# Layer boundaries run token tile by token tile, with the next features staged between the granules

## What is computed

```python
def rms_norm(x, w):
    y = xf * lax.rsqrt(jnp.mean(xf * xf, axis=-1, keepdims=True) + NORM_EPS)
    return (y * w.astype(jnp.float32)).astype(x.dtype)
...
h = x
for layer in range(DEPTH):
    u = rms_norm(h, mix_norm_pre[layer])
    u = even_mixer(u, ...) if layer % 2 == 0 else odd_mixer(u, ...)
    h = h + rms_norm(u, mix_norm_post[layer])
    u = swiglu(rms_norm(h, ffn_norm_pre[layer]), w_gate, w_up, w_down)
    h = h + rms_norm(u, ffn_norm_post[layer])
# second block: hn = rmsnorm(h, norm_gain[i]); proj = hn @ w_in[i] ...
```

## Time and profile before

| | us |
|---|---|
| median of 3 runs | 2949.03 (2949.02 to 2949.35) |
| the profiled execution, device time | 2949.33 |
| its span in the trace | 2947.5 |
| PE busy with matmuls | 2873.4 (97% of the span) |
| DVE busy | 1656.1 (56%) |
| ACT busy | 1409.6 (48%) |

### The profile page before, as it was taken

The page is one execution under the profiler, slowest core; times in us unless marked ns, Lnnn a source line. Parts: engine busy times, 40 slices in busy tenths (PEclk is TensorE's granted clock), DMA queues, the critical chain, the costliest instruction groups (busy, mean ns, idle before and its releaser), DMA issues.

```text
span 2947.5 us, 37450 instructions
## 1 busy us (share of the span) xinstructions
PE 2873.4 (97%) x15082; PEld 2379.9 (81%) x15082; DVE 1656.1 (56%) x2078; ACT 1409.6 (48%) x1802; POOL 25.2 (1%) x43
## 2 busy tenths in 40 slices
PE   8999989999999999999999999999999999999998
PEld 6888768788888888878887878888888887888886
DVE  5786855644544444564445554554444567786555
ACT  5554475544444444454446454444444445455444
POOL 0000000000000000000000000000000000000000
PEclk9999999999999999999999999999999999999999
DMA  6543325565555555555552655555555654444553
GB/s 238 174 142 114 115 100 202 171 200 188 185 193 192 190 195 185 190 171 197 186 188 83 199 184 191 190 187 192 193 189 190 204 186 139 149 151 170 194 176 129
DMA packets 255846, 516.84 MB, mean 175 GB/s; under 512 B 8528, under 2 KB 8752, under 8 KB 254688
## 3 DMA queue, kind: packets, MB, share of 16 engines
q1 hardware_dynamic: 252896, 501.61, 51.4%
q0 software_dynamic: 2816, 13.33, 1.4%
HBM read 511.76 MB, written 2.10 MB: 174 GB/s over the span
## 4 chain that ended last, share of the span: by engine, by line
PE 93%; DVE 4%; ACT 2%; issue 1%; DMA 0%; SPq 0%; ACTq 0%; DVEq 0%
PE acc L481 85%; DVE ar L1850 1%; ACT ar L1148 1%; PE side L548 1%; PE side L685 1%; PE side L678 1%; DVE wlo L1862 1%; PE side L807 1%; DVE ar L1853 1%; PE side L576 0%; DMA raw<-in_ev_w_in 0%; ACT L1148 0%; DVE u L1850 0%; PE side L951 0%; PE side L991 0%
## 5 line engine op out<-in xcount | busy, mean ns | idle before, releaser
L1862 DVE TENSOR_TENSOR wlo<-raw,whi 128x1024 fp32r<-128x1024 f32 x948 | 1154.4, 1224 | 1086.3 <-ACT whi L1159 1084.9
L1159 ACT ACTIVATE whi<-raw 128x1024 fp32r<-128x1024 f32 x948 | 998.5, 1060 | 1164.2 <-PE acc L481 1162.8
L481 PE MATMUL acc<-whi,xh 128*128 128x512 f32 x3008 | 823.7, 396 | 2.7 <-ACT whi L1159 2.5
L481 PE MATMUL acc<-wlo,xh 128*128 128x512 f32 x3008 | 806.5, 390 | 0.4
L481 PE MATMUL acc<-whi,xl 128*128 128x512 f32 x3008 | 806.5, 390 | 0.0
L481 PEld LDWEIGHTS acc<-wlo,xh 128*128 128x128 f32 x3008 | 564.9, 188 | 121.1 <-DVE wlo L1862 2.9
L481 PEld LDWEIGHTS acc<-whi,xl 128*128 128x128 f32 x3008 | 565.8, 188 | 119.9
L481 PEld LDWEIGHTS acc<-whi,xh 128*128 128x128 f32 x3008 | 555.8, 189 | 114.3 <-issue 3.3
L481 PE MATMUL acc<-whi,hTh 128*128 128x512 f32 x784 | 212.0, 392 | 0.0
L481 PE MATMUL acc<-wlo,hTh 128*128 128x512 f32 x784 | 209.8, 389 | 0.1
L481 PE MATMUL acc<-whi,hTl 128*128 128x512 f32 x784 | 209.6, 389 | 0.0
(11 more groups left out here) (267 smaller groups left out, 1265.7 us busy)
## 6 DMA issues: line engine op xcount, KB each, us to landing
raw<-in_ffn_w_gate SPq DMA_DIRECT2D x88, 1024.0 KB, 5.1
raw<-in_ffn_w_up SPq DMA_DIRECT2D x88, 1024.0 KB, 5.1
raw<-in_ffn_w_down SPq DMA_DIRECT2D x88, 1024.0 KB, 5.0
raw<-in_ev_w_in SPq DMA_DIRECT2D x56, 1024.0 KB, 5.1
raw<-in_od_w_in SPq DMA_DIRECT2D x48, 1024.0 KB, 5.1
raw<-in_w_in SPq DMA_DIRECT2D x32, 1024.0 KB, 5.2
raw<-in_ev_w_out SPq DMA_DIRECT2D x16, 1024.0 KB, 5.0
raw<-in_od_w_out SPq DMA_DIRECT2D x16, 1024.0 KB, 5.0
```

Source lines behind the costliest of these rows:

```text
L481: mm = pe.matmul(acc[2 * pair + t][:], x[:, k0 + j, t * P:t * P + P], w[:, ring, j], start=start and j == 0, stop=stop and j == 1)
L1159: act.activation(whi[:, place % RING], raw_granule(place), ACT.Copy).then_inc(S("hi_done"), 1)
L1862: dve.tensor_tensor(wlo[:, place % RING], raw_granule(place), whi[:, place % RING].bitcast(F32), ALU.subtract).then_inc(S("lo_done"), 1)
```

## The change

At the four boundaries:

- On PE the last two granules of the last chunk of ev_out, dn0b, od_out and dn1b are not run one after the other but as `by_tile`: all twelve matmuls of tile 0 (both granules, three sweeps of two), then all twelve of tile 1. Tile 0's end raises the new semaphore `tile_done`; tile 1's part raises `used` for each granule.
- ACT and DVE enter `lead` after the split of granule 1 of the user layer instead of granule 2 (`lead_at` 1). There the chain is run tile by tile: square, sum, root, reciprocal of tile 0, then h of tile 0 for chunks 0 and 1, then the same for tile 1. Only features of rounds 0 and 1 are made in `lead`.
- PE transposes tile 0 of rounds 0 and 1 on its own, then tile 1 (`open_stream`); rounds 2 and 3 stand before granule 1, rounds 4 and 5 before granule 3, rounds 6 and 7 before granule 4 (`STREAM_AT`, keys are PE's j).
- ACT makes the `xh` of those rounds after its splits of granules 2, 4 and 5 (j - 1 in `STREAM_AT`). DVE makes h of chunk 2 and the `xl` of rounds 4 and 5 after its split of granule 4, and h of chunk 3 and the `xl` of rounds 6 and 7 after its split of granule 5 (`rest`).
- A semaphore `ab_copied` is merged into `ab_done`, and counts of `ssum_done`, `rmsu_done`, `rstdu_done` are doubled, one for each tile.

The diff, cut to its core (s_in is done as od_in is, and feed_forward likewise):

```diff
@@ -76,6 +76,8 @@
 GATE_AT = {3: (0, 1), 4: (2,), 5: (3,), 6: (4,), 7: (5,)}
 LEAD = 7
 STATS = 5
+STREAM_AT = {1: (2, 3), 3: (4, 5), 4: (6, 7)}
+STREAM_READY = (3, 4, 6, 8)
...
+                        if name in POST and c == CHUNKS[name] - 1 and j >= per - 2:
+                            if j == per - 1:
+                                by_tile(name, pair, lhs_h, lhs_l)
+                            yield
+                            continue
                         granule(g, g % RING, pair, lhs_h, lhs_l, 2 * j, j == 0, j == per - 1, low)
                         yield
+
+            def by_tile(name, pair, lhs_h, lhs_l):
+                per = KTS[name] // 2
+
+                def sweep(n, t, x, w, stop=False):
+                    g = gran(name, CHUNKS[name] - 1, per - 2 + n)
+                    k0 = 2 * (per - 2 + n)
+                    for j in range(2):
+                        mm = pe.matmul(acc[2 * pair + t][:], x[:, k0 + j, t * P:t * P + P], w[:, g % RING, j],
+                                       start=False, stop=stop and j == 1)
+                    return mm
+
+                for t in range(TT):
+                    for n in range(2):
+                        g = gran(name, CHUNKS[name] - 1, per - 2 + n)
+                        if t == 0:
+                            pe.wait_ge(S("hi_done"), g + 1)
+                        sweep(n, t, lhs_h, whi)
+                        sweep(n, t, lhs_l, whi)
+                        if t == 0:
+                            pe.wait_ge(S("lo_done"), g + 1)
+                        mm = sweep(n, t, lhs_h, wlo, stop=n == 1)
+                        if t:
+                            mm.then_inc(S("used"), 1)
+                        elif n:
+                            mm.then_inc(S("tile_done"), 1)
...
-                        pe.wait_ge(S("h_done"), 8 * n + 2 * (r // 2) + 2)
+                        pe.wait_ge(S("h_done"), 8 * n + (STREAM_READY[r // 2] if n < 4 else 2 * (r // 2) + 2))
...
+            def open_stream(name, src):
+                n = ("up0a", "od_in", "up1a", "s_in").index(name)
+                base = 8 * TOF[name]
+                banks = [claim(side[r], "xl_done", 2 * (base + r) + 2) for r in range(2)]
+                for t in range(TT):
+                    pe.wait_ge(S("h_done"), 8 * n + (STREAM_READY[0] if t else 1))
+                    for k in range(4):
+                        mm = pe.transpose(banks[k // 2][:, k % 2 * TOK + t * P:k % 2 * TOK + t * P + P],
+                                          src[:, t, k * P:k * P + P], ident)
+                        if t and k % 2:
+                            mm.then_inc(S("tof_ready"), 1)
+
             def features_use(name, src=None):
 
                 def use(c, j):
                     if c == 0:
-                        if src is not None and j < 3:
+                        if name in ("up0a", "od_in", "up1a", "s_in"):
+                            if j == 0:
+                                open_stream(name, src)
+                            elif j in STREAM_AT:
+                                to_features(name, src, STREAM_AT[j])
+                        elif src is not None and j < 3:
                             to_features(name, src, (range(4), range(4, 6), range(6, 8))[j])
                         pe.wait_ge(S("xh_done"), 2 * (8 * TOF[name] + j + 1))
...
-            def granules(name, evac, lead, aside=None, after=2):
+            def granules(name, evac, lead, aside=None, after=2, lead_at=None):
...
-                        if j == min(after, per - 1):
-                            if c == 0:
-                                lead()
-                            else:
-                                evac(c - 1)
+                        if c == 0 and j == min(after if lead_at is None else lead_at, per - 1):
+                            lead()
+                        if c and j == min(after, per - 1):
...
-            def square_out(name, c):
+            def square_out(name, c, tiles=range(TT)):
                 n = 8 * POST[name] + 2 * c
-                if name[:2] != "dn":
-                    chunk_done(name, c)
                 pair = (CHUNK0[name] + c) % 2
-                for t in range(TT):
+                for t in tiles:
                     if name[:2] == "dn":
                         act.wait_ge(S("u_done"), 8 * int(name[2]) + 2 * c + t + 1)
                         src = u[:, t, c * CH:c * CH + CH]
                     else:
+                        if c == 3 and t == 0:
+                            act.wait_ge(S("tile_done"), POST[name] + 1)
+                        else:
+                            chunk_done(name, c)
                         src = acc[2 * pair + t][:]
                     if n + t:
                         act.wait_ge(S("sq_done"), n + t)
                     if n + t and POST[name] and c == 0:
-                        act.wait_ge(S("ssum_done"), POST[name])
+                        act.wait_ge(S("ssum_done"), 2 * POST[name])
                     run(at(14336, CH), src, ACT.Square, "sq_done", accum_out=ss[:, 4 * t + c:4 * t + c + 1])
...
-            def rms_out(name):
-                act.wait_ge(S("ssum_done"), POST[name] + 1)
-                if POST[name]:
-                    act.wait_ge(S("rstdu_done"), POST[name])
-                run(rms_u, ssum, ACT.Sqrt, "rmsu_done", scale=1.0 / DM, bias=EPS)
+            def roots_out(name, user):
+                before_root()
+                for t in range(TT):
+                    square_out(name, 3, (t,))
+                    act.wait_ge(S("ssum_done"), 2 * POST[name] + t + 1)
+                    if POST[name]:
+                        act.wait_ge(S("rstdu_done"), 2 * POST[name] + t - 1)
+                    run(rms_u[:, t:t + 1], ssum[:, t:t + 1], ACT.Sqrt, "rmsu_done", scale=1.0 / DM, bias=EPS)
+                features_hi(user, range(2))
...
-                            if first and m == 0 and j == 2:
+                            if first and m == 0 and j == (1 if name[3] == "a" else 2):
                                 lead()
+                            if first and m == 0 and name[3] == "a" and j - 1 in STREAM_AT:
+                                features_hi(name, STREAM_AT[j - 1])
...
-                    before_root()
-                    square_out(before, 3)
-                    rms_out(before)
-                    features_hi(f"up{l}a")
+                    roots_out(before, f"up{l}a")
...
+            def summed(name, c, t):
+                pair = (CHUNK0[name] + c) % 2
+                x = u[:, t, c * CH:c * CH + CH]
+                if c == 3 and t == 0:
+                    dve.wait_ge(S("tile_done"), POST[name] + 1)
+                else:
+                    chunk_done(name, c)
+                dve.wait_ge(S("half_done"), 8 * (int(name[2]) + 1))
+                tt(x, acc[2 * pair + t][:], x, ALU.add, "u_done")
+
+            def gained(name, c, tiles=range(TT)):
                 n = POST[name]
                 if n < 4 and c == 0:
                     dve.wait_ge(S("grow_in"), 16 * (n + 1))
@@ -2190,13 +2251,10 @@
                         dve.wait_ge(S("h_done"), 8 * n)
                 pair = (CHUNK0[name] + c) % 2
                 cl = slice(c * CH, c * CH + CH)
-                if name[:2] == "dn":
-                    l = int(name[2])
-                    chunk_done(name, c)
-                    dve.wait_ge(S("half_done"), 8 * (l + 1))
-                    for t in range(TT):
-                        tt(u[:, t, cl], acc[2 * pair + t][:], u[:, t, cl], ALU.add, "u_done")
-                for t in range(TT):
+                if name[:2] == "dn" and c < 3:
+                    for t in tiles:
+                        summed(name, c, t)
+                for t in tiles:
                     dve.wait_ge(S("sq_done"), 8 * n + 2 * c + t + 1)
                     src = u[:, t, cl] if name[:2] == "dn" else acc[2 * pair + t][:]
                     tt(u[:, t, cl], src, grow[:, cl], ALU.mult, "ug_done")
@@ -2204,24 +2262,48 @@
             def into_stream(name, user):
 
                 n = POST[name]
-                dve.wait_ge(S("sq_done"), 8 * n + 8)
-                if n:
-                    dve.wait_ge(S("rmsu_done"), n)
-                dve.tensor_reduce(ssum, ss.rearrange("p (t c) -> p t c", t=TT), AX_X, ALU.add)\
-                    .then_inc(S("ssum_done"), 1)
-                dve.wait_ge(S("rmsu_done"), n + 1)
-                dve.reciprocal(rstd_u, rms_u).then_inc(S("rstdu_done"), 1)
-                dve.wait_ge(S("rstdu_done"), n + 1)
-                dve.wait_ge(S("ug_done"), 8 * n + 8)
+
+                def root(t):
+                    if name[:2] == "dn":
+                        summed(name, 3, t)
+                    dve.wait_ge(S("sq_done"), 8 * n + 6 + t + 1)
+                    if n:
+                        dve.wait_ge(S("rmsu_done"), 2 * n - 1 + t)
+                    dve.tensor_reduce(ssum[:, t:t + 1], ss[:, 4 * t:4 * t + 4], AX_X, ALU.add).then_inc(S("ssum_done"), 1)
```

(56 more changed lines are left out.)

75 lines of the change are left out of this document (34 added, 41 removed).

## The result

| | us |
|---|---|
| median before, same chip | 2949.19 (2949.02 to 2951.3) |
| median after | 2972.24 (2968.62 to 2973.78) |
| ratio | 1.0071, interval 1.0059 to 1.0082 |
| span of the profiled execution | 2970.6, before 2947.5 |

The forecast was 2960.0 with a range of 2950 to 2968: right in sign and in where it happens, too low by 12 us and outside its range. First the page and PE's waits of the changed kernel (in it `granule` is line 483, `by_tile` 533, `to_features` 581, `open_stream` 592, DVE's helper for h and `xl` 1905, ACT's for `xh` 1198 and for `whi` 1209).

A forecast was written before the change was run, and what follows sets the result against it. PE was taken as busy nearly throughout, so only its boundary waits could pay. Shifts of +1.25, +2.4, +0.4 and +4.95 (+9.0), plus +2.1 for the clock, on the median 2949.0 gave 2960 us, range 2950 to 2968.

The forecast's parts named there:

- What bounds, and the yardstick: PE busy nearly throughout; boundaries measured by granule 7's start after Z, the last full sweep's end; each loses 6.4 to 8.0 us.
- The early chain: Tile 0's chain starts 2.73 us earlier; granule 0 starts at Z + 3.8 (ev_out, od_out) or Z + 5.6 (dn0b, dn1b).
- The moved h's: h of chunks 2 and 3, behind splits 4 and 5, makes PE wait before granules 3 and 4: 0.8 and 2.4 us first.
- `whi` at granule 6: At each boundary ACT's statistics delay split 6, so PE waits 1.2 us, plus 0.3 for `wlo`.
- The sum at full clock: Granule 7's shifts over the four boundaries, +1.25, +2.4, +0.4 and +4.95, together +9.0 us.
- The clock: Low clock after the stop in the two dn boundaries, 1.05 us each: +2.1, bounds 0 and +4.2.
- Rival (d): Clock falls again at granules 3 and 4 of each boundary, +1 to +2 each: 2964 to 2972 us, chance 0.12.
- (a): The gain survives, late h's come in time; boundaries at 25.5, 27.3, 25.5, 27.3: 2938 us, chance 0.10.
- (b): Break-even: half of the 0.8 + 2.4 + 1.5 per boundary is absorbed: about 2950 us, range 2944 to 2954, chance 0.15.
- the +13: Reading that transposes do not count as PE activity, so the low clock comes at every boundary.

The follow-up runs named there:

- after_warm: The changed kernel plus idle matmuls, whose results nobody reads, in PE's waits for h and first features at the boundaries: 2960.35 us, ratio 1.0031.
- h_early: The changed kernel with one move undone, h of chunks 2 and 3 made ahead of the split of granule 2: 2950.03 us, ratio 0.9994.
- before_again: The kernel before, run once more unchanged for its trace: 2951.27 us.
- early6_warm: h_early with the statistics one granule later and idle matmuls in the waits ahead of granule 0: 2941.71 us, ratio 0.9966; again 2941.85.
- before_warm: The kernel before with 18 or 21 idle matmuls in the one long wait for h at each boundary: 2944.82 us, ratio 0.998.
- after_again: The changed kernel, run once more unchanged: 2971.37 us, ratio 1.0065.

## Why the prediction was right, and where it was wrong

**What bounds, and the yardstick: right.** The work between boundaries did not move by 0.1 us.

**The early chain: right.** Granule 0 at Z + 3.8 and 5.6, in the trace 3.78, 5.74, 3.78, 5.74. The part of it that is `by_tile` is worth 7.5 us.

**The moved h's: right in place and size.** In the first and third boundary 0.8 + 2.4 were forecast, in the second 0.65 + 2.24; 0.48 + 2.06, 0.46 + 2.05 and 0.50 + 2.07 came in these three, and 2.50 + 2.34 in the fourth, where 2.65 + 4.1 were forecast. The 2.34 was short because granule 3 in front of it took 4.3 us at the low clock (its sweeps begin at 2479.12, the next granule's transposes wait from 2483.6) and DVE caught up meanwhile; with the clock held full, granule 7 of the fourth boundary is at 35.89, forecast 35.6. For `whi` at granule 6 1.2 were forecast and 1.07 came. The sum at full clock was +9.0; the four boundaries of after_warm have +9.6, single ones off by up to 0.3. h_early shows the cause by itself: 21 us back from moving four instructions of DVE in each boundary.

**The clock: this step failed, as a term of the sum.** It took +2.1, with bounds of 0 and +4.2: one fall behind the stop ahead of granule 0 in the two dn boundaries, 1.05 us each, and nothing anywhere else. The span of after's profile is 23.1 us over that of before, where the forecast had 11.1; it divides like this:

| | forecast | measured |
|---|---|---|
| boundaries at full clock (after_warm less before) | 9.0 | 9.6 |
| clock in the boundaries (after less after_warm) | 2.1 | 7.3 |
| outside the boundaries (after less before) | 0 | 6.2 |

In the first row before carries the clock loss of its own boundaries, and against before_again it would be 7.3. The forecast had the right place for most of the second row and the wrong price: the clock fell behind the stop in three boundaries instead of two, and a fall there cost 1.4 to 2.3 us, not 1.05; that is 6.0 of the 7.3. The falls behind the waits ahead of granules 3 and 4, taken at nothing, cost 1.4. The third row was taken at nothing as well, and it is half of the miss: the forecast compared with one execution of before in which the clock had held at places where it often falls, and the earlier trace rows, which was to show that a wait of 2.10 us is harmless, ends 0.1 us behind that wait. before_again has 1.00 in the same row and 0.68 over the next 5 us. Of the thirteen profiled executions without idle matmuls there, four show half clock in 205 to 210 us, and nine behind the wait of 2.05 us near 262 us.

Rival (d), 2964 to 2972, was given 0.12, and the measured 2972.24 is just past its end, but that is luck: it wanted falls at granules 3 and 4 of each boundary for 1 to 2 us each. There are four such falls in after, and they cost 1.4 us in all.

**The range: too narrow.** The kernel before was shown at three times within 0.33 us, over 23 later executions it lies between 2948.87 and 2954.09. The 6.2 us outside the boundaries stand in the granted clock. Ahead of the first boundary after falls at two places where before does not, shown here by two windows of after and one of before (for 205 to 210 before had 1.00, above). Traces with one fall, at one of these places or at the like one near 310 us, have Z at 559.6 to 559.9; before with none has 558.50, after with two 561.49:

```profile
205.00:210.00 5.00, 4.41 (x30) 4.02 (x31) 4.01 (x5) 0.60 (x1) 0.00 (x0) 0.66 0.12 11
262.00:270.00 8.00, 7.29 (x37) 6.42 (x38) 2.54 (x5) 2.14 (x3) 0.00 (x0) 0.79 0.00 1
```

```profile
262.00:270.00 8.00, 8.00 (x49) 7.01 (x48) 2.39 (x3) 2.19 (x4) 0.00 (x0) 1.00 0.13 24
```

Behind the last boundary after's code runs 19.9 us later than that of before. Two stretches of after, then the same work in before:

```profile
2505.00:2515.00 10.00, 10.00 (x149) 8.74 (x149) 6.95 (x12) 3.74 (x6) 3.85 (x8) 0.83 0.85 256
2570.00:2585.00 15.00, 15.00 (x261) 12.89 (x259) 9.18 (x16) 3.65 (x5) 0.00 (x0) 0.77 0.40 137
```

```profile
2485.00:2495.00 10.00, 10.00 (x149) 8.70 (x149) 6.95 (x12) 3.75 (x6) 3.94 (x8) 0.83 0.85 256
2550.00:2565.00 15.00, 15.00 (x273) 13.01 (x273) 11.62 (x21) 4.93 (x6) 0.00 (x0) 1.00 0.47 148
```

The first is as slow in before as in after; the second is what after has on top, and the 3.2 us are there. PE is busy all through both, so the windows say that it was slow, not why it became so.

**Rivals (a) and (b).** (a) did not come because h was late, as argued; its boundaries (25.5, 27.3, 25.5, 27.3) are nearly those of early6_warm, which puts h early and the statistics later. (b), half of the waits absorbed, did not come: they are there in full but for 0.3 each.

**Two rules that were weighed.** By the Trainium skill, page TensorE: Matmul & The Clock Gate, "Why this matters for your kernels", the clock would have stayed full behind gaps this short, which gave +9.0. The traces disagree: waits of 2.05 to 2.14 us were enough in some executions. The same page of the Trainium skill, "Part 4: PE-mode transpose", says that transposes do not count as PE activity in the same way, which gave the +13. Half clock behind each stop would have followed from it; after's first boundary stops for 1.75 and 0.77 with four transposes between, and the first sweep behind it takes 1.20 us, full clock (first fence of its timeline); its third boundary has the same pattern and half clock:

```profile
1716.59 0.66 PE L592 MATMUL side<-cc,h 128*128 128x128 f32 x4 [1.75 <-DVE h L1905]
1718.02 2.07 PE L483 MATMUL acc<-whi,xh 128*128 128x512 f32 x4 [0.77 <-ACT xh L1198]
```

Neither rule decides it.

**What stays open.** What makes the clock fall behind a wait of 2.1 us in one execution and not in the next; no kernel here changes that alone. What lies behind the last boundary was left unfilled, and whether the change itself makes the clock fall there more often is not shown: both profiles of after have 473.4 us, those of before 470.2 and 468.8.

## What to carry to other kernels

When a step is moved behind later work in a queue, count what stands in front of it there and compare with the time at which the consumer will ask; four cheap instructions behind two splits cost 21 us here. Cutting one long wait of PE into several short ones does not save the clock: allow 1.4 to 2.4 us, as measured here, for a fall behind each stop of some 3 us, and look at several executions, and at the stretch behind the wait, before a 1.00 is taken as a rule. A single profile of the kernel before can itself be a lucky one; 2.4 of the 23 us here were that (2949.19 against 2951.61). To find what the clock costs in a kernel, fill its waits with matmuls that nobody reads, fewer than fit into the wait, and compare landmarks within the traces, since the medians also move with stretches that were not filled.

## What the runs showed of the hardware

- The granted clock falls to the 1.2 GHz level behind waits of 2.05 to 2.14 us in some executions and stays at 2.4 GHz in others of the same kernel (1.00 and 0.68 over 205 to 210 us in before and before_again; four of thirteen executions at that wait).
- Idle matmuls in the waits hold it: 11.0 us back in after, 6.5 in before; no boundary of after_warm or before_warm has a stretch at the low clock.
- A fall behind the stop ahead of granule 0, with PE waiting for 2.5 to 3.8 us and doing eight transposes in it, cost 1.4 to 2.4 us (three boundaries each of after and after_again).
- A matmul of 128x512 on plain float32 operands shows as two of 0.43 us, one in fp32r as one of 0.23.
- Twelve matmuls of 512 columns in a row into one bank run at the usual pitch (0.45 us for two), so `by_tile` costs PE nothing.
